# Seven half-size products in place of eight for the forget and query projections and for the second gate

## The chip, the cores and the metric

The kernel runs on one core of one Trainium2 chip. The metric is device time in microseconds, the median of several runs; for the kernel before it is 1528.08 us over three runs (1526.75 to 1529.6).

## The reference

The reference is two layers of a streaming encoder. They work on 288 tokens, 256 of a prompt and 32 of a second request. What matters here is the combined projection at the head of each layer and what its parts feed:

```python
proj = x @ lp['w_in']                       # x: 288 x 1024
cq, ckv, kr, f_pre, q_pre, i_pre, g_pre, ga, gb = split(proj)
# widths: 384, 256, 32, 512 (f), 512 (q), 512 (i), 512 (g), 1024 (ga), 1024 (gb)
log_f = logaddexp(log(lb), log1p(-lb) + log_sigmoid(f_pre))
k = (1 - lb) * sigmoid(-f_pre);  q = silu(q_pre);  v = i_pre      # the recurrence's inputs
merged = sigmoid(ga) * (A @ w_br_a) + sigmoid(gb) * (B @ w_br_b)  # A attention, B recurrence
x = LN1(alpha * x + merged @ w_out)
x = LN2(alpha * x + hierarchical_moe(x) + sigmoid(x @ w_ple_gate) * (p @ w_ple))
```

All data are float32. After the mixers each layer has 32 experts, whose weights (three matrices of 1024 x 512 each) are all read from HBM.

## The kernel before

Every engine has one instruction stream written out by hand, and semaphores order them. A *job* is one filling of a PSUM bank: `tensor_jobs`, `gated_tensor_jobs`, `MIX_JOBS` and `expert_jobs` list the jobs in TensorE's order, and `Book` gives each a number and a bank (the first list goes round the 8 banks; in the second, the side jobs of the gates use banks 6 and 7 in turn). `job_done` waits until TensorE has finished a job, `job_read` until its bank has been emptied.

The normalised input stands turned in `xT` (128 partitions x 8 chunks x 288 tokens). Weights come in *pieces* of 1 MB (128 partitions x 4 chunks x 512 columns, half of the 1024 input rows by 512 outputs) into an 8-slot ring. SyncE issues their loads in the order of `weight_pieces`, each waiting for the last job that used the piece before it in the slot (`last_use`).

- **Forget and query** (f, q). Four jobs each, one for every 128 outputs: `by_features` runs 8 matmuls (the 8 chunks of input) of 128 x 128 weights with 288 tokens. ScalarE takes Sigmoid and Abs of f straight from the bank (L1693, L1694), then Exp and Ln; VectorE ends the logarithm (L2119); in the second layer more steps follow for the lower bound. q goes through Silu (L1726).
- **Gates** (ga, gb). Eight such jobs each. `GATE_AT` strews them between the jobs of the recurrence, where TensorE would otherwise wait: after which job of tile t they stand is the key. ScalarE copies each bank away (L1721), and before the branches `gate_values` takes the Sigmoid of two gates at a time.
- **Recurrence.** For tiles t = 0, 1, 2 VectorE builds decays by levels, and TensorE multiplies them, jobs ("A", t, j), then turns k ("ks", t), then makes the outputs ("o", t) and the new state ("Sn", t). VectorE empties these in tile order; L2292 to L2308 and `whole_products` (L2271 to L2273) stand at a tile's end.
- **Branches, mix, experts.** The branches multiply the gates (`mT`); w_out and the router follow. When the last chunk of `mT` is done (`mg_out`), SyncE starts to load expert weights into the arena, and from then on through the layer one load after another is issued as slots come free.

GpSimd issues the small transfers: norms, caches, the two mask rows of queries and keys (which wait for `lf_out`, since the scratch `fw` lies on the keys' place), states.

## Time and profile before

| | us |
|---|---|
| median of three runs | 1528.08 |
| lowest, highest | 1526.75, 1529.6 |
| the profiled execution, its own time | 1529.54 |
| span of its trace | 1527.7 |
| TensorE busy | 1284.0 (84%) |
| VectorE busy | 404.1 (26%) |
| ScalarE busy | 284.9 (19%) |
| GpSimd busy | 54.1 (4%) |

The span is the stretch from the first to the last instruction of the profiled core. PE is TensorE's matmuls, PEld its weight loads, DVE VectorE, ACT ScalarE, POOL GpSimd, SP SyncE. Every float32 matmul of the program makes two records in the trace: 8 matmuls of a gate job are 16 records. A row of the timeline merges neighbours of one kind, and its length runs to the end of the last; since matmuls are pipelined, the pace of a group is read from its start to the start of the next row.

### The profile page before, as it was taken

The numbers are of one execution on the slowest core, as the hardware profiler recorded it, in microseconds if no ns is written. First come the engines' busy times: TensorE is split into PE (matmuls) and PEld (weight loads), VectorE is DVE, ScalarE is ACT, GpSimd is POOL, SyncE is SP. The second block draws the span as 40 slices with busy tenths as digits, with TensorE's granted clock in tenths as the row PEclk, the third lists the DMA queues.
The fourth block names the chain that finished last, engine by engine and source line by source line (L and its number), as shares of the span: only waits on it lengthen the run. The fifth ranks groups of instructions, "written<-read, shape, count | busy, mean of one in ns | idle before, by whom it ended". The sixth has DMA issues, their size and how long they took to land.

```text
span 1527.7 us, 20304 instructions
## 1 busy us (share of the span) xinstructions
PE 1284.0 (84%) x8528; PEld 722.5 (47%) x8529; DVE 404.1 (26%) x1027; ACT 284.9 (19%) x712; POOL 54.1 (4%) x94
## 2 busy tenths in 40 slices
PE   6999999999787767766799999999997787667665
PEld 4766887554332323322276678876342323223211
DVE  4242643542111101011133536245311111011003
ACT  2342522021001101001044434312111011010001
POOL 1300000000000000000022010000000000000000
PEclk9999999999999878788899999999998988788778
DMA  9503435999999999999972043469999999999994
GB/s 332 162 3 111 173 117 181 386 371 430 430 429 429 430 430 430 430 429 428 383 250 84 6 148 130 179 231 410 369 429 430 431 431 429 431 427 432 430 424 183
DMA packets 79951, 488.78 MB, mean 320 GB/s; under 512 B 7344, under 2 KB 13424, under 8 KB 49776
## 3 DMA queue, kind: packets, MB, share of 16 engines
q1 hardware_dynamic: 75392, 476.47, 75.8%
q0 software_dynamic: 4464, 10.93, 2.3%
q8 instruction: 73, 1.20, 0.3%
q14 instruction: 22, 0.18, 0.0%
HBM read 484.48 MB, written 2.89 MB: 319 GB/s over the span
## 4 chain that ended last, share of the span: by engine, by line
PE 61%; DMA 33%; SPq 2%; DVE 2%; issue 1%; ACT 0%; POOL 0%; DVEq 0%
PE bank L1036 59%; DMA ring<-in_w_e_down 10%; DMA arena<-in_w_e_up 6%; DMA ring<-in_w_e_up 5%; DMA ring<-in_w_e_gate 5%; DMA arena<-in_w_e_gate 4%; DMA arena<-in_w_e_down 2%; PE bank L1086 2%; SPq L872 2%; DMA ring<-in_w_in 1%; DVE arena L2043 0%; SPq L933 0%; DVE x_sb L2052 0%; ACT xT L1644 0%; PE bank L1481 0%
## 5 line engine op out<-in xcount | busy, mean ns | idle before, releaser
L1036 PE MATMUL bank<-arena 128*32 128x512 f32 (+11 forms) x2808 | 570.6, 538 | 175.6 <-DMA ring<-in_w_e_up 51.0
L1036 PE MATMUL bank<-ring,arena 128*32 128x512 f32 (+4 forms) x1360 | 420.4, 647 | 33.4 <-DMA arena<-in_w_e_gate 15.4
L1036 PEld LDWEIGHTS bank<-arena 128*32 128x32 f32 (+6 forms) x2808 | 210.1, 137 | 442.2 <-issue 428.8
L1036 PE MATMUL bank<-ring,xT 128*32 128x128 f32 (+5 forms) x1536 | 237.7, 364 | 1.5 <-ACT xT L1644 1.1
L1036 PE MATMUL bank<-xT,ring 128*128 128x288 f32 x768 | 191.8, 407 | 0.0
L1036 PEld LDWEIGHTS bank<-ring,xT 128*32 128x32 f32 (+1 forms) x1536 | 121.7, 137 | 101.1 <-issue 90.9
L1036 PEld LDWEIGHTS bank<-ring,arena 128*32 128x32 f32 (+1 forms) x1360 | 108.0, 130 | 121.1 <-issue 114.4
L1036 PEld LDWEIGHTS bank<-xT,ring 128*128 128x128 f32 x768 | 143.7, 190 | 37.9
L1036 PE MATMUL bank<-arena,x_sb 128*128 128x128 f32 (+1 forms) x768 | 99.7, 282 | 1.4 <-DVE arena L2375 0.8
L1036 PEld LDWEIGHTS bank<-arena,x_sb 128*128 128x128 f32 (+1 forms) x768 | 90.5, 190 | 19.4 <-issue 12.7
L1036 PE MATMUL bank<-cst,arena 128*32 128x512 f32 x144 | 91.0, 792 | 0.0
L2548 DVE TENSOR_TENSOR arena<-arena,bank 128x512 f32<-128x512 f32 x16 | 11.0, 688 | 241.5 <-PE bank L1036 241.5
L1036 PE MATMUL bank<-arena,ring 128*128 128x288 f32 (+2 forms) x352 | 72.9, 372 | 0.0
L1036 PE MATMUL bank<-lb,arena 128*32 128x512 f32 x144 | 64.8, 592 | 0.0
L1036 PEld LDWEIGHTS bank<-arena,ring 128*128 128x128 f32 (+1 forms) x352 | 56.3, 180 | 14.8 <-issue 0.4
L2555 DVE COPY arena<-bank 128x512 f32<-128x512 f32 x16 | 11.1, 692 | 194.2 <-PE bank L1036 194.2
L1932 ACT COPY arena<-bank 128x512 f32<-128x512 f32 x16 | 9.4, 586 | 232.1 <-PE bank L1036 231.9
L2375 DVE TENSOR_TENSOR arena<-small,arena 128x128 f32<-128x128 f32 (+1 forms) x42 | 9.6, 283 | 147.7 <-PE bank L1036 147.7
L2485 DVE TENSOR_TENSOR arena<-arena,bank 128x512 f32<-128x512 f32 (+1 forms) x64 | 39.3, 630 | 23.2 <-PE bank L1036 23.2
L1985 ACT COPY arena<-bank 128x512 f32<-128x512 f32 x16 | 9.4, 587 | 172.6 <-PE bank L1036 172.6
L1969 ACT ACTIVATE arena<-bank 128x512 f32<-128x512 f32 x16 | 9.6, 597 | 156.1 <-PE bank L1036 156.1
L2421 DVE COPY arena<-bank 128x512 f32<-128x512 f32 x16 | 11.1, 692 | 80.3 <-PE bank L1036 80.3
(232 smaller groups left out, 878.4 us busy)
## 6 DMA issues: line engine op xcount, KB each, us to landing
arena<-in_w_e_up SPq DMA_DIRECT2D x30, 2048.0 KB, 28.2
arena<-in_w_e_gate SPq DMA_DIRECT2D x28, 2048.0 KB, 27.0
ring<-in_w_e_gate SPq DMA_DIRECT2D x24, 2048.0 KB, 25.6
arena<-in_w_e_down SPq DMA_DIRECT2D x20, 2048.0 KB, 23.7
ring<-in_w_e_down SPq DMA_DIRECT2D x18, 2048.0 KB, 25.1
ring<-in_w_in SPq DMA_DIRECT2D x32, 1024.0 KB, 8.7
ring<-in_w_e_up SPq DMA_DIRECT2D x16, 2048.0 KB, 24.0
arena<-in_w_e_gate SPq DMA_DIRECT2D x16, 1024.0 KB, 14.3
```

The costliest lines, as they stand in the source:

```text
L872: sp.dma_start(slot(n)[:, D * c:D * c + D], src).then_inc(last_full if c else ring_full[SLOT_OF[n]], 16)
L1036: return pe.matmul(out, lhsT, rhs, start=first, stop=last, skip_group_check=True)
L1086: ins = pe.transpose(b[0:m, a:a + src.shape[0]], src, ident[0:src.shape[0], 0:src.shape[0]])
L1932: emptied(act.copy(xeT[:, 0:4, :], bank(key)[:, :].rearrange("p (c t) -> p c t", c=4)), key)
L1969: emptied(act.activation(eh[:, :], bank(key)[:, :], ACT.Silu), key)
L1985: emptied(act.copy(ye[0], bank(key)[:, :]), key)
L2375: return dve.tensor_tensor(s4, bcast(places[0:n, :], 1, QUAD), bcast(ranks, 2, CAP), ALU.is_equal)
L2421: emptied(dve.tensor_copy(xeT[:, 4:8, :], bank(key)[:, :].rearrange("p (c t) -> p c t", c=4)), key)
L2485: emptied(dve.tensor_tensor(a, a, src, ALU.add), key)
L2548: emptied(dve.tensor_tensor(hid[:, :], eh[:, :], bank(key)[:, :], ALU.mult), key)
L2555: emptied(dve.tensor_copy(ye[1], bank(key)[:, :]), key)
```

## The change

For the pair f, q and for gb alone the product of a 2 x 2 block of weights (output half j, input half h) with a 2 x 2 block of tokens (token half i of 144, input half) is done in the Strassen-Winograd form, by seven products of half size instead of eight:

- VectorE makes four differences of token quarters after the input has been turned: `xb`, `xa`, `xd` and `xc` (in two parts), 576 elements a partition each. They lie in `lb` and in the free part of `lnw`, and both groups use them.
- Three products use weights as loaded (m = 4, 5, 3) and four use sums of pieces (m = 2, 1, 7, 6). Each product is two jobs (p = 0, 1) of 2 x 4 matmuls with 144 tokens.
- f and q: the four sums (2048 elements a partition each) are made by VectorE in the ring's slots, in place.
- gb: the four sums are made by transfers that add to their destination, issued by GpSimd: two from `w_in` in HBM, two from another slot of the ring. Each of the last three waits for the product that still reads the old content, and the last two wait for the sum before them.
- The products are gathered in SBUF. ScalarE copies m = 4 (twice), 5 and 3; VectorE then adds or subtracts the others' banks, one or two operations each (`gather`). Sigmoid, Abs and Silu work on the gathered f (`fz`) and q.
- ga's four pieces come before gb's four in the order of loads. The order of ScalarE's and VectorE's work after f and q is other: turned latents are read before the logarithm is ended. GpSimd's mask transfers no longer wait for `lf_out`.

The diff, cut:

```diff
+SEVEN = (4, 5, 3, 2, 1, 7, 6)
+SEVEN_WEIGHTS = {1: (1, 1), 2: (0, 0), 3: (1, 0), 4: (0, 0), 5: (1, 1), 6: (1, 0), 7: (0, 1)}
+SEVEN_LAST = {(0, 0): 1, (0, 1): 7, (1, 0): 6, (1, 1): 6}
+SUMS = (2, 7, 1, 6)
+SEVEN_TO = {5: ((0, 0, "subtract"),), 3: ((0, 1, "add"),), 2: ((1, 0, "add"), (1, 1, "subtract")),
+            7: ((0, 0, "add"),), 1: ((0, 0, "add"), (1, 1, "add")), 6: ((1, 1, "add"),)}
...
 GATE_AT = {("ss",): [("ga", 0), ("ga", 1)], ("lat",): [("ga", 2)],
            ("A", 0, 1): [("ga", 3)], ("A", 0, 3): [("ga", 4)], ("ks", 0): [("ga", 5)], ("o", 0): [("ga", 6)],
-           ("A", 1, 1): [("ga", 7)], ("A", 1, 3): [("gb", 0)], ("ks", 1): [("gb", 1)], ("o", 1): [("gb", 2)],
-           ("A", 2, 0): [("gb", 3), ("gb", 4)], ("ks", 2): [("gb", 5)], ("o", 2): [("gb", 6), ("gb", 7)]}
+           ("A", 1, 1): [("ga", 7)], ("A", 1, 3): seven_of("gb", 4), ("ks", 1): seven_of("gb", 5), ("o", 1): seven_of("gb", 3),
+           ("A", 2, 0): seven_of("gb", 2, 1), ("ks", 2): seven_of("gb", 7), ("o", 2): seven_of("gb", 6)}
...
-    for j in range(2):
-        out += [("ga", j, 0), ("ga", j, 1), ("gb", j, 0), ("gb", j, 1)]
+    out += [(name, j, h) for name in ("ga", "gb") for j in range(2) for h in range(2)]
...
-    j += [(name, h) for name in ("f", "q") for h in range(HH)]
+    j += seven_of("fq", *SEVEN)
...
-        return (name, HH - 1)
+        return ("fq", SEVEN_LAST["fq".index(name), key[1]], 1)
...
+        def quarter(i, k):
+            return xT[:, 4 * k:4 * k + 4, S * i:S * i + S]
...
+        xa = tiles(lbr[:, 40:40 + 4 * S])
+        xb = tiles(lbr[:, 40 + 4 * S:40 + 8 * S])
+        xc_parts = [tiles(lbr[:, 40 + 8 * S:40 + 10 * S]), tiles(early[:, 4 * T:4 * T + 2 * S])]
+        xd = tiles(early[:, 4 * T + 2 * S:4 * T + 6 * S])
+        whole = lambda a: [a[:, c, :] for c in range(4)]
+        seven_tokens = {1: whole(xa), 2: whole(quarter(1, 1)), 3: whole(quarter(0, 0)), 4: whole(xb), 5: whole(quarter(0, 1)),
+                        6: [part[:, c, :] for part in xc_parts for c in range(2)], 7: whole(xd)}
+        def seven_out(name, i, j, p):
+            pair = gate_pair(FEATURES // 2 + 2 * j + p).rearrange("p (u t) -> p u t", u=2) if name == "gb" else (fz, hqT)[j][:, 2 * p:2 * p + 2, :]
+            return pair[:, :, S * i:S * i + S]
...
-                pool.wait_ge(lf_out, 2 * layer + 2)
...
+                ns = {(j, h): piece_number(layer, ("gb", j, h)) for j in range(2) for h in range(2)}
+                w = {at: slot(n).rearrange("p (c n) -> p c n", c=4) for at, n in ns.items()}
+                def from_input(j, h):
+                    a = OFF["gb"][0] + 512 * j
+                    return w_in[layer].rearrange("(p c) n -> p c n", c=8)[:, 4 * h:4 * h + 4, a:a + 512]
                 job_read(pool, (layer, "aTs"))
                 pool.dma_start(state[1][:, :, :], state_hgrn[layer, 0].rearrange("h k v -> k h v")).then_inc(state_in, 16)
+                pool.wait_ge(ring_full[SIGNAL_OF[ns[0, 1]]], 16 * FILLS[ns[0, 1]])
+                pool.dma_start(w[0, 1], from_input(1, 1), accum_op=ALU.add).then_inc(gb_sum[7], 16)
+                job_done(pool, (layer, "gb", 4, 1))
+                pool.dma_start(w[0, 0], from_input(0, 1), accum_op=ALU.add).then_inc(gb_sum[2], 16)
+                job_done(pool, (layer, "gb", 5, 1))
+                pool.wait_ge(gb_sum[2], 16 * (layer + 1))
+                pool.dma_start(w[1, 1], w[0, 0], accum_op=ALU.add).then_inc(gb_sum[1], 16)
+                job_done(pool, (layer, "gb", 3, 1))
+                pool.wait_ge(gb_sum[1], 16 * (layer + 1))
+                pool.dma_start(w[1, 0], w[1, 1], accum_op=ALU.add).then_inc(gb_sum[6], 16)
...
+                def seven(key, n):
+                    m, p = key[-2:]
+                    arrived(n)
+                    pe.wait_ge(forms_out, layer + 1)
+                    if key[1] == "gb" and m in SUMS:
+                        pe.wait_ge(gb_sum[m], 16 * (layer + 1))
+                    if key[1] == "fq" and m in SUMS:
+                        pe.wait_ge(fq_sums, 4 * layer + SUMS.index(m) + 1)
+                    w = slot(n).rearrange("p (c n) -> p c n", c=4)
+                    b = open_bank(key)
+                    for u in range(2):
+                        f = 2 * p + u
+                        for c in range(4):
+                            ins = mm(b[:, S * u:S * u + S], w[:, c, P * f:P * f + P], seven_tokens[m][c], c == 0, c == 3)
+                    done(ins)
...
-                for name in ("f", "q"):
-                    for h in range(HH):
-                        by_features(layer, (name, h), h, [(name, 0), (name, 1)], xT)
+                for name, m, p in seven_of("fq", *SEVEN):
+                    j, h = SEVEN_WEIGHTS[m]
+                    seven((layer, name, m, p), piece_number(layer, ("fq"[j], h)))
...
-                for h in range(HH):
-                    job_read(pe, (layer, "q", h))
+                pe.wait_ge(hq_out, layer + 1)
...
+                def seven_copies(key, signal):
+                    name, m, p = key[1:]
                     job_done(act, key)
-                    z = bank(key)[:, 0:T]
-                    act.activation(hk[:, h, :], z, ACT.Sigmoid, scale=-1.0)
-                    ins = act.activation(lf[:, h, :], z, ACT.Abs)
-                step(ins)
+                    if m == 4:
+                        act.copy(seven_out(name, 0, 0, p), seven_bank(key))
+                        emptied(act.copy(seven_out(name, 1, 0, p), seven_bank(key)), key)
+                    else:
+                        act.copy(seven_out(name, 0 if m == 5 else 1, 1, p), seven_bank(key)).then_inc(signal, 1)
+                for key in seven_of("fq", 4, 5, 3):
+                    seven_copies((layer,) + key, fq_copied)
+                act.wait_ge(fq_out, 2 * layer + 1)
+                act.activation(hk[:, :, :], fz[:, :, :], ACT.Sigmoid, scale=-1.0)
+                step(act.activation(lf[:, :, :], fz[:, :, :], ACT.Abs))
...
+                act.wait_ge(fq_out, 2 * layer + 2)
+                act.activation(hqT[:, :, :], hqT[:, :, :], ACT.Silu).then_inc(hq_out, 1)
...
+                step(dve.tensor_tensor(xb, quarter(1, 0), quarter(1, 1), ALU.subtract))
+                step(dve.tensor_tensor(xa, quarter(0, 0), xb, ALU.subtract))
+                dve.tensor_tensor(xd, quarter(0, 1), xa, ALU.subtract)
+                dve.tensor_tensor(xc_parts[0], quarter(1, 0)[:, 0:2, :], quarter(0, 0)[:, 0:2, :], ALU.subtract)
+                dve.tensor_tensor(xc_parts[1], quarter(1, 0)[:, 2:4, :], quarter(0, 0)[:, 2:4, :], ALU.subtract).then_inc(forms_out, 1)
+                def gather(key, signal):
+                    name, m, p = key[1:]
+                    job_done(dve, key)
+                    if m in (5, 3):
+                        dve.wait_ge(signal, copied(layer, m, p))
+                    job_read(dve, (layer, name, SEVEN[SEVEN.index(m) - 1], p))
+                    for i, j, op in SEVEN_TO[m]:
+                        g = seven_out(name, i, j, p)
+                        ins = dve.tensor_tensor(g, g, seven_bank(key), {"add": ALU.add, "subtract": ALU.subtract}[op])
+                    return emptied(ins, key)
...
+                js = {(j, h): piece_number(layer, ("fq"[j], h)) for j in range(2) for h in range(2)}
+                for n in (js[0, 1], js[1, 1]):
+                    dve.wait_ge(ring_full[SIGNAL_OF[n]], 16 * FILLS[n])
+                w = {at: slot(n) for at, n in js.items()}
+                job_done(dve, (layer, "fq", 4, 1))
+                dve.tensor_tensor(w[0, 0], w[0, 0], w[0, 1], ALU.add).then_inc(fq_sums, 1)
+                dve.wait_ge(fq_sums, 4 * layer + 1)
+                dve.tensor_tensor(w[0, 1], w[0, 1], w[1, 1], ALU.add).then_inc(fq_sums, 1)
+                gather((layer, "fq", 5, 0), fq_copied)
+                gather((layer, "fq", 5, 1), fq_copied)
+                dve.wait_ge(fq_sums, 4 * layer + 2)
+                dve.tensor_tensor(w[1, 1], w[0, 0], w[1, 1], ALU.add).then_inc(fq_sums, 1)
+                gather((layer, "fq", 3, 0), fq_copied)
+                gather((layer, "fq", 3, 1), fq_copied)
+                dve.wait_ge(fq_sums, 4 * layer + 3)
+                dve.tensor_tensor(w[1, 0], w[1, 0], w[1, 1], ALU.add).then_inc(fq_sums, 1)
+                for m in (2, 1, 7, 6):
+                    for p in range(2):
+                        gather((layer, "fq", m, p), fq_copied)
+                    if m in (7, 6):
+                        for p in range(2):
+                            job_read(dve, (layer, "fq", m, p))
+                        dve.sem_inc(fq_out, 1)
...
+                    gates_at("A", t, j)
...
+                    gates_at("ks", t)
+                    gates_at("o", t)
```

Where the orders differ. First TensorE at the start of f and q; a row is line, operation, output bank <- operands, size, and the semaphores waited for. Before:

```order
L1036 MATMUL bank<-xT,ring 128x288 [waits ring_full4,bank_emptied4]
L1036 MATMUL bank<-xT,ring 128x288 x3
L1036 MATMUL bank<-xT,ring 128x288 [waits ring_full5]
L1036 MATMUL bank<-xT,ring 128x288 x3
L1036 MATMUL bank<-xT,ring 128x288 [waits ring_full4,bank_emptied5]
L1036 MATMUL bank<-xT,ring 128x288 x3
```

In the changed kernel, from the second job of m = 4 to the first of m = 2 (`lb` holds xb; forms_out is the token differences, fq_sums VectorE's sums of weights):

```order
L1105 MATMUL bank<-lb,ring 128x144 [waits bank_emptied5,forms_out,ring_full4]
L1105 MATMUL bank<-lb,ring 128x144 x7
L1105 MATMUL bank<-xT,ring 128x144 [waits bank_emptied6,forms_out,ring_full7]
L1105 MATMUL bank<-xT,ring 128x144 x7
L1105 MATMUL bank<-xT,ring 128x144 [waits bank_emptied7,forms_out,ring_full7]
L1105 MATMUL bank<-xT,ring 128x144 x7
L1105 MATMUL bank<-xT,ring 128x144 [waits bank_emptied0,forms_out,ring_full6]
L1105 MATMUL bank<-xT,ring 128x144 x7
L1105 MATMUL bank<-xT,ring 128x144 [waits bank_emptied1,forms_out,ring_full6]
L1105 MATMUL bank<-xT,ring 128x144 x7
L1105 MATMUL bank<-xT,ring 128x144 [waits fq_sums,bank_emptied2,forms_out,ring_full4]
L1105 MATMUL bank<-xT,ring 128x144 x7
```

A job of 8 matmuls with 288 tokens has become a job of 8 with 144. From m = 2 on (the first row with fq_sums) a product waits for a sum. The first list of jobs is six longer now, so its banks shift: ("A", 0, 0), the first job of the second list, takes the bank that ("g", 2), two jobs earlier, has filled; before it was the bank of ("ga", 2).

VectorE at the same place. Before, after the third tile's latents it had four operations for f and then the turned latents:

```order
L2102 SCALAR_TENSOR_TENSOR arena<-arena,small 32x256 [waits kr_out]
L2119 SCALAR_TENSOR_TENSOR arena<-bank,arena 128x288 [waits f_act]
L2119 SCALAR_TENSOR_TENSOR arena<-bank,arena 128x288
L2119 SCALAR_TENSOR_TENSOR arena<-bank,arena 128x288 [waits bank_emptied4,bank_emptied5,f_act]
L2119 SCALAR_TENSOR_TENSOR arena<-bank,arena 128x288
L2145 COPY arena<-bank 128x3x128 [waits bank_emptied6,bank_emptied7,matmuls_done]
```

Now the four sums over `ring` stand there, with the gathers between them:

```order
L2229 SCALAR_TENSOR_TENSOR arena<-arena,small 32x256 [waits kr_out]
L2246 TENSOR_TENSOR ring<-ring 128x2048 [waits matmuls_done,ring_full7,ring_full5]
L2248 TENSOR_TENSOR ring<-ring 128x2048 [waits fq_sums]
L2213 TENSOR_TENSOR arena<-arena,bank 128x2x144 [waits bank_emptied4,fq_copied,matmuls_done]
L2213 TENSOR_TENSOR arena<-arena,bank 128x2x144 [waits bank_emptied5,fq_copied,matmuls_done]
L2252 TENSOR_TENSOR ring<-ring 128x2048 [waits fq_sums]
L2213 TENSOR_TENSOR arena<-arena,bank 128x2x144 [waits bank_emptied6,fq_copied,matmuls_done]
L2213 TENSOR_TENSOR arena<-arena,bank 128x2x144 [waits bank_emptied7,fq_copied,matmuls_done]
L2256 TENSOR_TENSOR ring<-ring 128x2048 [waits fq_sums]
L2213 TENSOR_TENSOR arena<-arena,bank 128x2x144 [waits bank_emptied0,matmuls_done]
L2213 TENSOR_TENSOR arena<-arena,bank 128x2x144
L2213 TENSOR_TENSOR arena<-arena,bank 128x2x144 [waits bank_emptied1,matmuls_done]
```

The first sum waits for a matmul job (m = 4 done) and for two pieces; each gather waits for its product and for ScalarE's copy.

TensorE at the second gate, between the recurrence's ("Sn", 1) and ("A", 2, 0). Before, two gate jobs:

```order
L1036 MATMUL bank<-xT,ring 128x288 [waits ring_full2,bank_emptied6]
L1036 MATMUL bank<-xT,ring 128x288 x3
L1036 MATMUL bank<-xT,ring 128x288 [waits ring_full3]
L1036 MATMUL bank<-xT,ring 128x288 x3
L1036 MATMUL bank<-xT,ring 128x288 [waits ring_full6,bank_emptied7]
L1036 MATMUL bank<-xT,ring 128x288 x3
L1036 MATMUL bank<-xT,ring 128x288 [waits ring_full7]
L1036 MATMUL bank<-xT,ring 128x288 x3
```

Now the products m = 2 and m = 1, two jobs each, in banks 7, 6, 7, 6:

```order
L1105 MATMUL bank<-xT,ring 128x144 [waits gb_sum_2,bank_emptied7,forms_out,ring_full4]
L1105 MATMUL bank<-xT,ring 128x144 x7
L1105 MATMUL bank<-xT,ring 128x144 [waits gb_sum_2,bank_emptied6,forms_out,ring_full4]
L1105 MATMUL bank<-xT,ring 128x144 x7
L1105 MATMUL bank<-lb,ring 128x144 [waits gb_sum_1,bank_emptied7,forms_out,ring_full7]
L1105 MATMUL bank<-lb,ring 128x144 x7
L1105 MATMUL bank<-lb,ring 128x144 [waits gb_sum_1,bank_emptied6,forms_out,ring_full7]
L1105 MATMUL bank<-lb,ring 128x144 x7
```

The third job wants the bank that the first of them filled: VectorE must have gathered it. gb_sum_2 and gb_sum_1 are the adding transfers.

## Rows read from the trace of the kernel before

**Rows 1.** the page's part 4, shares of the chain that ended last

```profile
PE 61%; DMA 33%; SPq 2%; DVE 2%; issue 1%; ACT 0%; POOL 0%; DVEq 0%
PE bank L1036 59%; DMA ring<-in_w_e_down 10%; DMA arena<-in_w_e_up 6%; DMA ring<-in_w_e_up 5%; DMA ring<-in_w_e_gate 5%; DMA arena<-in_w_e_gate 4%; DMA arena<-in_w_e_down 2%; PE bank L1086 2%; SPq L872 2%; DMA ring<-in_w_in 1%; DVE arena L2043 0%; SPq L933 0%; DVE x_sb L2052 0%; ACT xT L1644 0%; PE bank L1481 0%
```

**Rows 2.** stretches A:B; length, busy us of PE and others, then PE clock, DMA share, GB/s

```profile
38.50:69.64 31.14, 31.14 (x133) 24.43 (x129) 3.84 (x14) 12.40 (x26) 12.47 (x24) 1.00 0.44 134
409.00:768.00 359.00, 261.00 (x1717) 107.17 (x1710) 50.10 (x98) 33.55 (x60) 0.00 (x0) 0.85 1.00 424
```

**Rows 3.** timeline of SP, which issues the weight loads: start, us, transfers

```profile
269.65 5.10 SPq L806 DMA_DIRECT2D arena<-in_w_e_gate  x8
```

**Rows 4.** timeline of PE: start us, us, engine, line, operation, tiles, shape, count

```profile
38.50 31.31 PE L1036 MATMUL bank<-xT,ring 128*128 128x288 f32 x128
69.64 2.60 PE L1086 MATMUL bank<-cst,arena 128*128 128x128 f32 x18
...
98.28 2.02 PE L1036 MATMUL bank<-arena 98*128 98x128 f32 x16 [0.36 <-DVE arena L2167]
...
165.54 3.68 PE L1036 MATMUL bank<-arena 128*128 128x64 f32 x32
169.06 4.10 PE L1036 MATMUL bank<-xT,ring 128*128 128x288 f32 x16
...
183.73 2.84 PE L1036 MATMUL bank<-arena 128*128 128x128 f32 x24
186.41 3.80 PE L1036 MATMUL bank<-xT,ring 128*128 128x288 f32 x15
```

**Rows 5.** timeline of PE, first layer, where the second gate's jobs stand

```profile
194.25 4.05 PE L1036 MATMUL bank<-xT,ring 128*128 128x288 f32 x16
...
200.57 4.15 PE L1036 MATMUL bank<-xT,ring 128*128 128x288 f32 x16
...
211.55 7.93 PE L1036 MATMUL bank<-xT,ring 128*128 128x288 f32 x32
...
225.78 7.93 PE L1036 MATMUL bank<-xT,ring 128*128 128x288 f32 x32
233.64 3.13 PE L1036 MATMUL bank<-arena 32*32 32x128 f32 x24
```

**Rows 6.** timeline of VectorE, whose additions and outputs stand beside those jobs

```profile
32.21 0.61 DVE L2093 SCALAR_TENSOR_TENSOR arena<-arena,small 32x384 f32<-32x384 f32 x1 [1.44 <-ACT small L1630]
...
212.60 1.13 DVE L2292 SCALAR_TENSOR_TENSOR arena<-bank,small,arena 128x128 f32<-128x128 f32 x4 [9.99 <-ACT small L1630]
...
215.93 0.28 DVE L2273 TENSOR_TENSOR arena<-arena 128x128 f32<-128x128 f32 x1
...
240.33 0.46 DVE L2322 TENSOR_TENSOR xT<-lnw,bank 128x288 f32<-128x288 f32 x1
...
817.00 0.76 DVE L2137 TENSOR_TENSOR arena<-arena 128x576 f32<-128x576 f32 x1 [1.23 <-ACT arena L1707]
```

**Rows 7.** timeline of all engines at the last jobs of the attention

```profile
159.73 1.11 ACT L1713 ACTIVATE arena<-bank 32x128 f32<-32x128 f32 x4 [1.33 <-PE bank L1036]
160.66 0.97 PEld L1036 LDWEIGHTS bank<-arena 128*128 128x128 f32 x8
```

**Rows 8.** DMA issues of three stretches: line, queue, count, KB each, median us to landing

```profile
ring<-in_w_in SPq DMA_DIRECT2D x4, 1024.0 KB, 8.1
...
ring<-in_w_ple_gate SPq DMA_DIRECT2D x2, 1024.0 KB, 6.4
lnw<-in_ln_g POOLq DMA_DIRECT2D x1, 512.0 KB, 4.5
arena<-in_p_prompt POOLq DMA_DIRECT2D x1, 256.0 KB, 3.0
...
ring<-in_w_in SPq DMA_DIRECT2D x4, 1024.0 KB, 10.3
arena<-in_state_hgrn POOLq DMA_DIRECT2D x1, 256.0 KB, 6.9
```

More of the change, by code:

```diff
@@ L319, in last_use @@
         return (name,) + LATE_PLAIN[3]
-    if name in ("ga", "gb", "bra", "brb"):
+    if name == "gb":
+        return (name, SEVEN_LAST[key[1:]], 1)
+    if name in ("ga", "bra", "brb"):
         return (name, 4 * key[1] + 3)
@@ L509, in build @@
         hg = carve(H + 6144, 3, 512)
+        fz = carve(H + 6144, HH, T)
         squares = carve(0, 512)
@@ L667, in build @@
         more_read = sem("more_read")
+        forms_out = sem("forms_out")
+        fq_sums = sem("fq_sums")
+        fq_copied = sem("fq_copied")
+        fq_out = sem("fq_out")
+        hq_out = sem("hq_out")
+        gb_sum = {m: sem(f"gb_sum_{m}") for m in SUMS}
+        gb_copied = sem("gb_copied")
         block = ctx.enter_context(nc.Block())
@@ L684, in bank, with seven_bank, copied @@
             return banks[book.bank(key)]
+        def seven_bank(key):
+            return bank(key)[:, 0:T].rearrange("p (u t) -> p u t", u=2)
+        def copied(layer, m, p):
+            return 4 * layer + 2 * (m == 3) + p + 1
         def further_passes(eng, layer, turn, body, each_pass=None):
@@ L1700, in _ @@
                     act.activation(z, z, ACT.Ln, bias=1.0).then_inc(f_act, 1)
+                for t in range(3):
+                    key = (layer, "kvT", t)
+                    job_done(act, key)
+                    src = bank(key)[:, 0:256].rearrange("p (c t) -> p c t", c=2)[:, :, 0:NT[t]]
+                    emptied(act.copy(ckvT[:, :, T0[t]:T0[t] + NT[t]], src), key)
                 if layer == 1:
@@ L2095, in _, with gates_at @@
                 for t in range(3):
+                    job_read(dve, (layer, "tx", t, 1))
+                step(dve.tensor_tensor(xb, quarter(1, 0), quarter(1, 1), ALU.subtract))
[13 more added lines that the diff above has]
+                    return emptied(ins, key)
+                def gates_at(*place):
+                    for name, *f in GATE_AT.get(place, []):
+                        if name == "gb" and f[0] != 4:
+                            gather((layer, name, *f), gb_copied)
+                for t in range(3):
                     key = (layer, "kv", t)
@@ L2133, in _ @@
-                if layer == 1:
-                    for i in range(2):
-                        z = lf[:, 2 * i:2 * i + 2, :]
-                        dve.wait_ge(f_add, i + 1)
-                        dve.tensor_tensor(z, z, fw[:, 2 * i:2 * i + 2, :], ALU.add).then_inc(lf_out, 1)
-                    dve.wait_ge(lf_out, 2 * layer + 2)
+                js = {(j, h): piece_number(layer, ("fq"[j], h)) for j in range(2) for h in range(2)}
+                for n in (js[0, 1], js[1, 1]):
+                    dve.wait_ge(ring_full[SIGNAL_OF[n]], 16 * FILLS[n])
@@ L2273, in whole_products @@
                     dve.tensor_tensor(ksufT[:, :, 0:n], ksufT[:, :, 0:n], hk[:, :, now(t)], ALU.mult).then_inc(ksuf_out, 1)
-                for h in range(HH):
-                    job_read(dve, (layer, "q", h))
+                dve.wait_ge(hq_out, layer + 1)
                 dve.wait_ge(zeroed, 3 * layer + 4)
```

85 lines of the change are left out of this document (46 added, 39 removed).

## The prediction

> **What bounds the kernel now.** I read the page's chain first. It gives 61% of the span to TensorE and 33% to transfers, nearly all of them expert weights [rows 1]. The two do not mix: they are stages. Then the stretches: from 409 to 768 us, in the experts, the DMA share is 1.00 at 424 GB/s while TensorE is busy for 261 of 359 us; at the f and q projections (38.50 to 69.64) TensorE is busy for all 31.14 us at granted clock 1.00 and the DMA share is 0.44 [rows 2]. So the dense stages are TensorE's and the expert stages the transfers'. What links them is the point from which expert weights are issued, 269.65 us in the first layer [rows 3], which follows the last chunk of the merged gates, so TensorE's dense work. Whatever the dense work before it loses, the stream starts earlier by, and as it then runs without a gap, the layer ends earlier by as much. The second layer is alike. A microsecond of TensorE saved in f, q or gb is therefore worth a microsecond.
>
> **Products.** 64 matmuls with 288 tokens, 128 records, take 69.64 - 38.50 = 31.14 us for f and q [rows 4], 243 ns a record. That is 288 columns at two cycles of 2.4 GHz (240 ns) and some 3 ns. A gate job of 16 records has the same pace (225.78 to 233.64 for two jobs, 7.86 us; I use 3.88 a job) [rows 5]. So eight gate jobs are 8 x 3.88 = 31.0 us. Afterwards each is 7 x 2 x 8 = 112 matmuls with 144 tokens, 224 records.
>
> The trace has no 144-column matmul. With so few columns the weight load (128 columns) could bound it, so I look at its floor: 32 records of 64 columns take 169.06 - 165.54 = 3.52 us, 110 ns each, though 64 columns alone would be 53; 24 records of 128 columns take 186.41 - 183.73 = 2.68 us, 112 ns [rows 4]. The loads run beside the matmuls and bound them at about 111 ns. 144 columns want 120 + 3 = 123 ns, which is above it. So 224 x 123 = 27.5 us. I take that; the lower bound of the saving is the case that an overhead appears (a rival below). The f/q group saves 31.14 - 27.5 = 3.6 us, gb 31.0 - 27.5 = 3.5 us, per layer.
>
> The Trainium skill says otherwise: in "TensorE: Matmul & The Clock Gate", section "Back-to-back issue gap", a stream of load and matmul pairs is paced by both, 81 ns at N = 128 against 56 for the matmul alone, 25 ns more; and the section on the array's mechanism lets a load overlap only with other row groups. By it, as an estimate, a record here is 123 + 25 = 148 ns, a group 33.2 us, and seven products lose 2 us against eight. The trace disagrees: at 128 columns its records stand 112 ns apart where two cycles a column alone are 107.
>
> **f and q: what must be hidden.** Each product m takes 32 x 123 = 3.9 us: from 38.5, m = 4 ends at 42.4, 5 at 46.4, 3 at 50.3, 2 at 54.2, 1 at 58.1, 7 at 62.1, 6 at 66.0.
> - *Token differences.* 576 elements cost VectorE 0.76 us, 288 about 0.45 [rows 6]: 3 x 0.76 + 2 x 0.43, some 3.3 us with their waits. They follow the operation that ends at 32.82 [rows 6] and end near 36.2, before 38.5. Cost 0, spare 2.3 us; beyond that TensorE waits.
> - *Weight sums.* 2048 elements by the slope from 288 to 576 elements (0.46, 0.76: about 1.05 ns an element) are 2.3 us. Two start when m = 4 is done: 42.5 to 47.1. The first is wanted at 50.3. Two gathers, then the third, 48.1 to 50.4, wanted at 54.2. The fourth, 51.3 to 53.6, wanted at 62.1. Each has at least 3.8 us to spare. In the second layer the steps of the lower bound stand ahead of the first sum, a few operations and two waits for ScalarE; its 5.5 us should hold them. Cost 0 in both.
> - *Gathers.* 12 jobs of one or two additions at 0.46: each job's work is under 1 us against 1.96 us of its matmuls; the banks come round after eight jobs. Cost 0.
> - *The logarithm.* f is whole only after m = 7, 4 us before the group's end, where half of it was read before. ScalarE's chain on it (in the second layer the longer one) now runs beside the turned latents, i and the query's up-projection, whose copies queue behind it on ScalarE. TensorE has 98.28 - 69.64 = 28.6 us of jobs before the first scores [rows 4], and ScalarE only these copies. Cost 0; if that fails, what is late are the first scores, where VectorE's copies of the keys stand in between anyway. I allow 1 us a layer.
>
> **gb: two new kinds of wait.** *VectorE as the one that empties banks.* Until m = 2 each product has a slot as long as a gate job had, so TensorE's times stay: m = 4 from 194.25, 5 from 200.6, 3 from 205, 2 from 211.6. Its first job is done at 213.6, and the first job of m = 1 wants the bank back at 215.6. But VectorE works at the outputs of tile 1 from 212.60 until 216.21 [rows 6], and the gather stands behind that: two additions, 217.1. TensorE waits 1.5 us. Behind the waiting job are ("A", 2, 0) and all that follows. No other gather is late.
> *The shifted bank.* ("A", 0, 0) now wants the bank of ("g", 2), which ScalarE empties at 159.73 + 1.11 = 160.84 [rows 7]; TensorE starts that job at 160.66 now [rows 7]. 0.2 us.
> *The adding transfers.* Let T be the time from issue to landing of one. Three form a chain: from m = 4's end (198.2) for m = 2 (wanted 211.6), then for m = 1 (217.1), then for m = 6 (226 + 1.5 = 227.5). The first needs T up to 13.4; two need 2T up to 18.9; three, 3T up to 29.3. So T up to 9.4 us costs nothing. The trace has no such transfer. Bounds: a plain 1 MB issued by SP lands after 6.4 to 10.3 us where several queue; GpSimd's 256 KB lands after 3.0, its 512 KB after 4.5 us [rows 8], which by their slope is 7.5 us for a plain 1 MB. Far above lies its 256 KB in 6.9 us among the gate's own loads [rows 8]; four times that is 27.6. Below: at the 424 GB/s of [rows 2] the data take 2.5 us and some 2.3 us are fixed, 4.8. An adding transfer also reads its destination, 2.5 us more: 7.3. I take 7.5, near the rows for 256 and 512 KB, which no queue held up. So no wait.
> The Trainium skill ("Collectives: The Full Stack", "The bandwidth ceiling: the fold count and why AG ≠ RS ≠ AR") says that the add itself costs nothing but that there are two source reads, which halve the rate; as an estimate that is the same 7.3 us, and no row here shows it.
>
> **Sum.** Per layer 3.6 + 3.5 - 1.5 - 0.2 = 5.4; both layers, 10.8 us. The profiled execution took 1529.54 us (its span 1527.7), 1.5 above the median of the runs. 1529.54 - 10.8 = 1518.7; against the median, 1528.08 - 10.8 = **1517.3 us**.
>
> **Rivals.**
> 1. *The adding transfers are the bound; slower.* Past T = 9.7 the last sum is late by 3T - 29.3 in each layer. The kernel is as before when this eats 5.4 us: T = 11.6. At T = 14 it waits 12.7 us a layer: 1528.1 - 10.8 + 25.4 = 1543. For it: GpSimd's 6.9 us for 256 KB; nobody here has seen adding. Against it: the bus has room there (TensorE's stage at f and q had a DMA share of 0.44 [rows 2], and no expert load runs), and the 3.0 us. 0.21 for T over 11, of which 0.02 up to 12.
> 2. *144 columns pay an overhead; no difference.* At 135 ns a record (12 over my figure) a group is 30.2 us and saves 0.8 to 0.9; with the waits, 4 x 0.85 - 3.4 = 0. 1528. For it: the load's floor is only 12 ns below. Against it: the 112 ns. 0.07. The page's 148 ns would give 1528.1 + 8.4 + 3.4 = 1540; 0.02.
> 3. *The bank wait does not come*, since gathers find VectorE free: 1517.3 - 3.0 = 1514.3. Against it stands VectorE's written order. 0.08.
> 4. *The stream does not follow*: the experts' start is bound elsewhere and the gain is lost in part. 1523. The trace has no gap to lose it in. 0.05.
> The forecast itself, with T up to 11: 0.57.
>
> **Numbers.** A difference under 0.2%, 3 us, could not be told from none. The forecast, rivals 3 and 4 are faster: 0.70. Rival 2 and T from 11 to 12 are the same: 0.09. Rival 1 beyond T = 12 and the page's pace are slower: 0.21. The range: down to 1513 (all waits gone), up to 1533 (T about 12.6); about 0.15 lies above and 0.04 below. The forecast's own range is 1514 to 1521.
>
> **What would show it.** Records with 144 columns 122 to 124 ns apart; f and q in 27.5 us with TensorE never idle for `fq_sums`; an idle of about 1.5 us before the first job of m = 1, ended by VectorE; adding transfers landing after about 7.5 us, with no idle ended by them; the first expert load 5.4 us earlier in the first layer and 10.8 in the second. It is wrong if TensorE idles for `gb_sum`, if records stand 135 ns apart, or if the second layer's scores wait for ScalarE.

## The result, and the profile after

The changed kernel takes 1517.59 us, the median of four runs (1516.82 to 1520.38), against 1528.57 for the kernel before on the same chip. The medians lie 10.98 us apart; the ratio of the runs is 0.9933 (95% 0.9919 to 0.9947), which is 10.2 us less (8 to 12). The forecast was 1517.3. The profiled execution took 1517.23 us, its span is 1515.5.

**The page.** Busy time, queue 0 (GpSimd's) and the chain:

```profile
PE 1273.6 (84%) x8912; PEld 738.4 (49%) x8913; DVE 453.6 (30%) x1109; ACT 287.0 (19%) x710; POOL 62.8 (4%) x102
...
q0 software_dynamic: 7152, 19.32, 5.4%
...
PE 57%; DMA 35%; DVE 3%; SPq 3%; issue 1%; ACT 1%; POOL 0%; DVEq 0%
```

TensorE is busy 10.4 us less than before and VectorE 49.5 more. TensorE's share of the chain fell from 61% to 57% [rows 1]. It is still the same chain of stages.

**f and q.** TensorE, start and length of merged groups (m = 4; then 5, 3 and 2 in one row; 1; 7; and m = 6 in small rows):

```profile
37.38 4.19 PE L1105 MATMUL bank<-lb,ring 128*128 128x144 f32 x32
41.41 11.92 PE L1105 MATMUL bank<-xT,ring 128*128 128x144 f32 x96
53.16 4.08 PE L1105 MATMUL bank<-lb,ring 128*128 128x144 f32 x32
57.09 4.08 PE L1105 MATMUL bank<-lnw,ring 128*128 128x144 f32 x32
61.01 0.65 PE L1105 MATMUL bank<-lb,ring 128*128 128x144 f32 x4
...
64.92 1.30 PE L1155 MATMUL bank<-cst,arena 128*128 128x128 f32 x9
```

From 37.38 to 64.92 are 27.54 us for 224 records, 123 ns each, where 128 records took 31.14 [rows 4]. No row has an idle time in brackets.

**The same stretches as [rows 2].** Length, busy time of each engine, granted clock, DMA share, GB/s:

```profile
37.38:64.92 27.54, 27.54 (x230) 27.54 (x225) 17.19 (x29) 9.29 (x21) 12.45 (x24) 1.00 0.53 156
...
409.00:768.00 359.00, 261.69 (x1719) 110.00 (x1719) 53.03 (x101) 34.41 (x63) 0.00 (x0) 0.85 1.00 422
```

**gb.** TensorE, the rows that answer to [rows 5]; in brackets the idle time and what ended it:

```profile
189.82 4.09 PE L1105 MATMUL bank<-lb,ring 128*128 128x144 f32 x32
193.74 2.50 PE L1105 MATMUL bank<-arena 128*128 128x64 f32 x24
196.17 4.19 PE L1105 MATMUL bank<-xT,ring 128*128 128x144 f32 x32
...
207.23 4.09 PE L1105 MATMUL bank<-xT,ring 128*128 128x144 f32 x32
212.77 4.16 PE L1105 MATMUL bank<-lb,ring 128*128 128x144 f32 x32 [1.45 <-DVE arena L2213]
```

The one wait of gb's products is that before m = 1, in the second layer as well:

```profile
957.61 4.16 PE L1105 MATMUL bank<-lb,ring 128*128 128x144 f32 x32 [1.45 <-DVE arena L2213]
```

VectorE at that place, with the outputs of tile 1 (L2443), the state (L2459), the products for tile 2 (L2423), and only then the gathers (L2213), as [rows 6] had it without the last:

```profile
208.28 1.13 DVE L2443 SCALAR_TENSOR_TENSOR arena<-bank,small,arena 128x128 f32<-128x128 f32 x4 [2.58 <-ACT small L1718]
...
210.05 1.11 DVE L2459 SCALAR_TENSOR_TENSOR arena<-arena,small,bank 128x128 f32<-128x128 f32 x4
...
211.62 0.28 DVE L2423 TENSOR_TENSOR arena<-arena 128x128 f32<-128x128 f32 x1
211.82 1.54 DVE L2213 TENSOR_TENSOR arena<-arena,bank 128x288 f32<-128x288 f32 x4
```

**The adding transfers.** GpSimd, the issues for m = 2, 1 and 6 of the first layer and of the second. An issue whose idle time was ended by a DMA started when the sum before it had landed:

```profile
194.33 1.28 POOL L1064 DMA_DIRECT2D ring<-in_w_in  x1 [28.14 <-PE bank L1105]
203.59 0.87 POOL L1067 DMA_DIRECT2D ring<-ring  x1 [7.98 <-DMA ring<-in_w_in]
211.11 0.84 POOL L1070 DMA_DIRECT2D ring<-ring  x1 [6.64 <-DMA ring<-ring]
...
939.19 1.30 POOL L1064 DMA_DIRECT2D ring<-in_w_in  x1 [27.15 <-PE bank L1105]
948.79 0.88 POOL L1067 DMA_DIRECT2D ring<-ring  x1 [8.29 <-DMA ring<-in_w_in]
956.98 0.84 POOL L1070 DMA_DIRECT2D ring<-ring  x1 [7.31 <-DMA ring<-ring]
```

From issue to next issue one link takes 9.26 and 7.52 us in the first layer, 9.60 and 8.19 in the second. From issue to landing it is 8.6 and 6.9, then 8.9 and 7.6; the 0.6 to 0.7 us between are GpSimd's hand-over to the next link. The sum for m = 1 was there at 211.1 and 957.0, against the starts of m = 1 at 212.77 and 957.61. So 1.7 and 0.6 us were left. Without VectorE's wait TensorE would have been ready 1.45 us sooner, at 211.32 and 956.16, so in the second layer the transfer hides behind that wait.

The fourth adding transfer, for m = 7, is off the chain: issued at 164.86 us among SyncE's plain loads of the ring, it landed after 13.6 us (14.5 in the second layer). Its issue, and the GB/s of 170 to 180 us in 40 slices:

```profile
ring<-in_w_in POOLq DMA_DIRECT2D x1, 1024.0 KB, 13.6
...
GB/s 262 262 262 262 262 262 262 262 262 262 262 262 262 262 262 254 287 246 262 262 262 254 246 254 262 254 254 262 254 262 320 385 418 393 426 401 410 385 254 82
```

Beside it the queues moved some 260 GB/s, and about 400 from 177.6 us on, when it was nearly done. Here nobody waited: m = 7 is wanted at 218.92.

**Where the time went.** I cut the span at six events: the start of f and q, the start of the branches and the first expert load, in either layer. From branches to load are 32.94 or 32.95 us in every case. The runs come from several chips, and each ratio is to the kernel before on the same chip, whose median there is 1528.51 to 1529.23 us. All kernels in one table (stretches in us, worked out from the starts of their rows, as 230.36 - 37.38 = 192.98):

| kernel | f/q starts | f/q to branches, layer 0 | load to layer 1's f/q | f/q to branches, layer 1 | last load point to end | median | ratio to before (95%) |
|---|---|---|---|---|---|---|---|
| before | 38.50 | 198.20 | 518.87 | 198.36 | 507.88 | 1528.57 | |
| changed | 37.38 | 192.98 | 518.80 | 193.08 | 507.36 | 1517.59 | 0.9933 (0.9919 to 0.9947) |
| fq_only | 37.86 | 194.87 | 518.83 | 194.97 | 506.77 | 1520.75 | 0.9945 (0.9932 to 0.9959) |
| gb_only | 37.12 | 196.29 | 519.16 | 196.29 | 505.75 | 1522.37 | 0.9957 (0.9944 to 0.9969) |
| early_gather | 37.19 | 191.75 | 519.04 | 191.93 | 505.79 | 1515.41 | 0.9913 (0.9899 to 0.9927) |
| early_gather_7first | 36.97 | 191.29 | 517.47 | 191.40 | 507.17 | 1512.29 | 0.9897 (0.9881 to 0.9912) |
| vector_sums_early | 37.42 | 191.74 | 517.62 | 191.83 | 508.50 | 1515.36 | 0.9915 (0.9902 to 0.9929) |
| sum1_twice | 37.48 | 201.05 | 517.82 | 201.08 | 506.07 | 1532.62 | 1.0020 (1.0009 to 1.0032) |
| sum6_twice | 37.14 | 200.06 | 520.87 | 200.93 | 505.61 | 1531.14 | 1.0013 (1.0004 to 1.0023) |

The two dense stretches give back 5.22 and 5.28 us, 10.5 together. The stretch that ends in the experts is as long as before (518.87, 518.80): the stream follows one for one. SyncE's first expert load answers to [rows 3]:

```profile
263.31 4.30 SPq L858 DMA_DIRECT2D arena<-in_w_e_gate  x8
...
1008.14 4.96 SPq L858 DMA_DIRECT2D arena<-in_w_e_gate  x8
```

6.3 us earlier than before, and 11.7 in the second layer (1019.82 before). Of both, 1.1 us is the earlier start of f and q. Without it they are 5.2 and 10.6, for 5.4 and 10.8 forecast. The start lies between 36.97 and 37.86 in the eight other traces of the table, and at 38.50 only in that of before. All of the 1.1 us arises before the latents of the second tile, which start at 21.73 us before and at 20.62 after; from there to f and q it is 16.77 and 16.76. No edited line runs that early, so I don't count it as the change's.

### The profile page after: what moved, and what is told of

Read it like the earlier page. It is cut to its first block, busy times and chain, and to the rows that moved or that the text cites. A ratio compares the mean times of both kernels' runs of the same rounds, so it can differ in the third digit from the quotient of the medians.

```text
span 1515.5 us, 21258 instructions
## 1 busy us (share of the span) xinstructions
PE 1273.6 (84%) x8912; PEld 738.4 (49%) x8913; DVE 453.6 (30%) x1109; ACT 287.0 (19%) x710; POOL 62.8 (4%) x102
## 4 chain that ended last, share of the span: by engine, by line
PE 57%; DMA 35%; DVE 3%; SPq 3%; issue 1%; ACT 1%; POOL 0%; DVEq 0%
PE bank L1105 55%; DMA ring<-in_w_e_up 7%; DMA ring<-in_w_e_down 5%; DMA ring<-in_w_e_gate 5%; DMA arena<-in_w_e_up 4%; DMA cst<-in_w_e_down 4%; DMA arena<-in_w_e_gate 4%; DMA cst<-in_w_e_gate 3%; DMA arena<-in_w_e_down 2%; SPq L924 2%; PE bank L1155 2%; DMA ring<-in_w_in 1%; SPq L985 0%; DVE arena L2304 0%; DVE arena L2144 0%
## 5 line engine op out<-in xcount | busy, mean ns | idle before, releaser
L1105 PE MATMUL bank<-xT,ring 128*128 128x144 f32 (+1 forms) x640 | 113.4, 335 | 0.0
L1105 PEld LDWEIGHTS bank<-xT,ring 128*128 128x128 f32 x640 | 95.1, 190 | 12.3
L2706 DVE COPY arena<-bank 128x512 f32<-128x512 f32 x16 | 11.1, 692 | 191.5 <-PE bank L1105 191.5
L1105 PE MATMUL bank<-lb,ring 128*128 128x144 f32 x320 | 43.5, 287 | 2.9 <-DVE arena L2213 2.9
L1105 PEld LDWEIGHTS bank<-lb,ring 128*128 128x128 f32 x320 | 40.7, 190 | 3.5 <-issue 3.3
```

The lines of the kernel that those rows point to most:

```text
L1105: return pe.matmul(out, lhsT, rhs, start=first, stop=last, skip_group_check=True)
L2706: emptied(dve.tensor_copy(ye[1], bank(key)[:, :]), key)
```

## The experiments

**One group alone.** fq_only gives gb back to `by_features`, with its order of loads; gb_only gives f and q back.

```diff
-("A", 1, 3): seven_of("gb", 4), ("ks", 1): seven_of("gb", 5), ...
+("A", 1, 3): [("gb", 0)], ("ks", 1): [("gb", 1)], ...        # fq_only
...
-    j += seven_of("fq", *SEVEN)
+    j += [(name, h) for name in ("f", "q") for h in range(HH)]  # gb_only
```

> Seven products for f and q alone; the gate gb is as in the kernel before. Theory (each part pays by its matmul time): f and q again in 27.5 us, 3.6 us less a layer, minus the 0.2 us of the shifted bank: 1528.1 - 6.8 = 1521.3 us, the first expert load 3.4 us earlier in layer 0 and 6.8 in layer 1. Rival (the 1.1 us by which f and q started earlier in the changed kernel's trace, 37.38 against 38.50, belong to the change): f and q start at 37.4 here too and the time is 1520.2. Rival (the gate carries the gain): above 1524.

> Seven products for the gate gb alone, with the adding transfers; f and q are as in the kernel before. Theory: 3.5 us less a layer, minus 1.5 us in which the first product of m = 1 waits for VectorE: 1528.1 - 4.0 = 1524.1 us. With the f and q run this adds up to the changed kernel's 11. Rival (the adding transfers take as much from the loads of the later weights as the products save): 1528. Rival (f and q carry nothing, the gate all): 1517.5.

Measured: 1520.75 and 1522.37 us. The dense stretches are shorter by 3.33 and 3.39 us (fq_only) and by 1.91 and 2.07 (gb_only). Added up that is 5.24 and 5.46, where the whole change has 5.22 and 5.28: the parts are independent, and each is worth its matmul time less its wait. In fq_only 0.25 of the 3.6 is missing, which is the shifted bank; TensorE idles there for 0.25 and 0.24 us in its two layers, as in this row of the changed kernel:

```profile
156.26 1.13 PE L1105 MATMUL bank<-arena 128*128 128x128 f32 x8 [0.25 <-ACT arena L1816]
```

In gb_only the wait for VectorE is the same. The idle time is 1.46 us; from start to start the step takes 5.55 us (215.82 - 210.27) where one without a wait takes 3.93, 1.6 more, and 3.5 - 1.6 is the 1.9 measured:

```profile
215.82 4.16 PE L1106 MATMUL bank<-lb,ring 128*128 128x144 f32 x32 [1.46 <-DVE arena L2219]
```

The early start of f and q is in gb_only too (37.12), whose f and q are the old ones, so it is not theirs. By time the two kernels gain 8.5 and 6.9 us against the median of their chip, 1529.23, more together than the change's 11.0, and gb_only's interval (4.7 to 8.6 us) leaves its 4.0 out. The surplus lies in the start (1.4 us) and after the last load point (2.1 us), where the edit changed nothing that I can name. One trace of the kernel before doesn't tell whether it is scatter; that stays open.

**The wait for VectorE taken away.**

```diff
-                        if name == "gb" and f[0] != 4:
+                        if name == "gb" and f[0] != 4 and f != [2, 0]:
...
                     dve.tensor_tensor(osb[0:n, :], osb[0:n, :], hg[0:n, t, :], ALU.mult).then_inc(o_out, 1)
+                    if t == 1:
+                        gather((layer, "gb", 2, 0), gb_copied)
                     key = (layer, "Sn", t)
```

> The changed kernel, but VectorE gathers the first half of product m = 2 before it updates the state of tile 1 instead of after it (0.8 us of work moved ahead). This takes away the wait of 1.45 us that each layer has before m = 1. Theory (behind that wait stands the chain of adding transfers, which lands for m = 1 at about 211.1 us in layer 0 and 957.0 in layer 1, while TensorE is ready at 211.3 and 956.2): the wait goes in layer 0, and in layer 1 some 0.8 us of it stay, now ended by the transfer: 1517.6 - 2.1 = 1515.5 us. Rival (VectorE is all there is to the wait): 1517.6 - 2.9 = 1514.7, no wait ended by a transfer. Rival (what follows on TensorE waits for VectorE anyway): 1517.6.

TensorE at m = 1, in both layers:

```profile
210.96 2.12 PE L1105 MATMUL bank<-lb,ring 128*128 128x144 f32 x16
213.31 2.20 PE L1105 MATMUL bank<-lb,ring 128*128 128x144 f32 x16 [0.23 <-DVE arena L2213]
...
955.28 4.16 PE L1105 MATMUL bank<-lb,ring 128*128 128x144 f32 x32 [0.33 <-DMA ring<-ring]
```

1515.41 us; the stretches lose 1.23 and 1.15. In the second layer the wait is now the transfer's, 0.33 us (0.8 expected). In the first, 0.23 stays for the second half's gather. The theory stands: behind the one wait stood another. By time alone the gain isn't clear of noise: this interval (0.9899 to 0.9927) and the changed kernel's (0.9919 to 0.9947) overlap a little. The two waits in the traces carry the reading.

**Another order, which gives the chain room.**

```diff
+GB_SEVEN = (4, 5, 3, 7, 2, 1, 6)
-("A", 2, 0): seven_of("gb", 2, 1), ("ks", 2): seven_of("gb", 7),
+("A", 2, 0): seven_of("gb", 7, 2), ("ks", 2): seven_of("gb", 1),
```

The gather moved ahead is that of m = 7, and gates of the first half wait for m = 1 in place of 7.

> The early gather kernel with another order of the gate's products: 4, 5, 3, 7, 2, 1, 6 in place of 4, 5, 3, 2, 1, 7, 6. The sum for m = 7 is ready long before, so each sum of the chain of adding transfers is wanted a product (3.9 us and more) later. Theory (in layer 1 what was left of the wait, 0.33 us, was the chain's): no wait ended by a transfer in either layer; from the start of f and q to the branches 191.8 us in layer 0 (as with the early gather) and 191.6 in layer 1 (191.9 there); 1515.1 us. Rival (the order is no matter, TensorE waits for VectorE's gathers alone): 191.8 and 191.9. Rival (m = 1 now stands where VectorE is late with the attention's last parts): a new wait of a microsecond, 1517.

```profile
206.83 4.09 PE L1106 MATMUL bank<-lnw,ring 128*128 128x144 f32 x32
...
952.57 4.08 PE L1106 MATMUL bank<-xT,ring 128*128 128x144 f32 x32
```

No wait is left between gb's products in either layer: 191.29 and 191.40 us, 0.5 and 0.2 under the theory. It had left the first layer's wait for VectorE in place, and that went too: a gather of m = 7 is one addition where m = 2 has two, so VectorE is done with the second half at 212.22 us, before TensorE wants the bank, and not at 213.16. 1512.29 us; the interval (0.9881 to 0.9912) lies below that of the change (0.9919 to 0.9947). It is the fastest of all, and beats both kernels; against the early gather the intervals overlap, and of the 3.1 us between the medians 1.0 is in the dense stretches. Of the 5.3 us against the changed kernel 3.4 are in the dense stretches; 1.3 are in the first layer's experts. That stretch runs from 517.47 to 520.87 us in the table, though no edit touches it, so the 1.3 are put down to scatter.

**The sums on VectorE.** The early gather with gb's sums made in the slots by VectorE:

```diff
-                pool.dma_start(w[1, 1], w[0, 0], accum_op=ALU.add).then_inc(gb_sum[1], 16)
...
+                                dve.tensor_tensor(gw[to], gw[a], gw[b], ALU.add).then_inc(gb_sum[m], 1)
```

> The early gather kernel with the gate's four weight sums on VectorE, between its gathers, in place of adding transfers. Theory (the transfers cost nothing where they land in time, and VectorE has gaps of 1.5 to 2.6 us between the gathers that hold most of 2.3 us a sum): the stretch from f and q to the branches is 191.4 to 191.9 us in both layers, 1515 us, the same as the early gather. Rival (the transfers take bandwidth from the loads beside them): shorter, 1513. Rival (four sums of 2.3 us in VectorE's order make the recurrence's steps late): TensorE waits 1 to 2 us a layer, ended by VectorE, 1518.

The first of VectorE's sums, behind a gather (L2195); the others are alike:

```profile
198.95 0.45 DVE L2195 TENSOR_TENSOR arena<-arena,bank 128x288 f32<-128x288 f32 x1 [0.35 <-ACT arena L1767]
199.32 2.28 DVE L2218 TENSOR_TENSOR ring<-ring 128x2048 f32<-128x2048 f32 x1
```

1515.36 us, stretches of 191.74 and 191.83 against 191.75 and 191.93: the same. So the transfers cost no time where they land in time. They do take from the loads beside them, as that rival had it: SyncE's two pieces of `w_br_a`, issued at 161 us, land after 18.6 us in the early gather kernel and after 13.7 here:

```profile
ring<-in_w_br_a SPq DMA_DIRECT2D x2, 1024.0 KB, 18.6
...
ring<-in_w_br_a SPq DMA_DIRECT2D x2, 1024.0 KB, 13.7
```

TensorE doesn't wait for them in either kernel, so the 5 us don't show in the stretches. VectorE had room for four sums, and is the surer place: all eight took 2.28 us.

**The chain made longer.** The transfer for m = 1 twice, then in another kernel that for m = 6:

```diff
                 pool.dma_start(w[1, 1], w[0, 0], accum_op=ALU.add).then_inc(gb_sum[1], 16)
+                pool.wait_ge(gb_sum[1], 32 * layer + 16)
+                pool.dma_start(w[1, 1], w[0, 0], accum_op=ALU.add).then_inc(gb_sum[1], 16)
...
```

> The changed kernel with the adding transfer for m = 1 issued twice, one behind the other (so the sum for m = 1 holds one piece twice). The chain is one transfer longer. Theory (a transfer lands 7.2 to 9.4 us after its issue, and the chain has under 2 us to spare before m = 1): the sum lands at about 218.5 in layer 0 and 964.5 in layer 1, and TensorE, which starts m = 1 at 212.8 and 957.6, waits some 6 more us in each; m = 6 waits for nothing more: 1517.6 + 12 = 1530 us. Rival (there is slack of a whole transfer, as my forecast of 7.5 us and 9.7 at most would have it in part: 3 x 7.5 = 22.5 against 18.9): + 3.6 us a layer, 1524.8. Rival (the second one costs only its data's time, 5 us): 1517.6 + 2 x 3.5 = 1524.6.

```profile
218.13 6.97 PE L1107 MATMUL bank<-lb,ring 128*128 128x144 f32 x32 [6.73 <-DMA ring<-ring]
...
970.85 6.10 PE L1107 MATMUL bank<-lb,ring 128*128 128x144 f32 x32 [7.53 <-DMA ring<-ring]
```

The theory has the waits (m = 1 starts 5.3 and 6.0 us later in its stretch than in the changed kernel), but 1532.62 us is 2.6 above its 1530. The same 32 records that took 4.16 us now take 6.97 and 6.10. The stretches say why (the column before the last two is the granted clock):

```profile
218.13:225.03 6.90, 6.90 (x32) 6.76 (x32) 0.82 (x2) 0.00 (x0) 1.64 (x2) 0.58 0.79 157
225.03:231.40 6.37, 6.37 (x89) 6.27 (x89) 2.95 (x10) 0.59 (x1) 0.00 (x0) 1.00 0.62 205
```

After 6.7 us of idleness the granted clock is 0.58 over the product, so TensorE was for the most part at its lower level, 1.2 GHz, and at 2.4 again (1.00) in the next stretch. So of the 8.07 us by which the first layer's dense stretch is longer than the changed kernel's, 5.3 are the wait and 2.8 the clock.

> The changed kernel with the last adding transfer, the one for m = 6, issued twice, one behind the other (so the sum for m = 6 holds one piece twice). In the changed kernel its issue stands at 211.1 us in layer 0 and 957.0 in layer 1 and it lands some 7.3 us later, where TensorE wants it at 223.3 and 968.1. Theory (the last sum has 4.9 and 3.8 us to spare): it lands at 225.8 and 971.7, TensorE waits 2.5 and 3.6 us ended by the transfer, and if so short a wait leaves the granted clock at 1.00 the time is 1517.6 + 6.1 = 1523.7 us. Rival (the clock falls as in the run with the transfer for m = 1 doubled, where 16 records of a product took about twice their time): + 2 us and more a layer, 1528. Rival (the last sum has a whole transfer's room): 1517.6.

```profile
227.69 1.30 PE L1107 MATMUL bank<-lb,ring 128*128 128x144 f32 x4 [4.35 <-DMA ring<-ring]
...
232.57 0.65 PE L1107 MATMUL bank<-lnw,ring 128*128 128x144 f32 x4
```

```profile
227.69:232.57 4.88, 4.88 (x20) 4.88 (x21) 0.46 (x1) 0.00 (x0) 0.00 (x0) 0.51 0.45 172
```

Here the theory failed and its rival was right, and still too low: 1531.14 us, 13.5 above the changed kernel. TensorE waited 4.35 and 5.64 us where 2.5 and 3.6 were expected, since the second of the two landed after 8.9 and 9.2 us where the first took 7.6 and 7.2. Beside the second ran a 256 KB store and SyncE's loads of `w_out` (the row is the first layer's); that they made it late is likely but not shown by a run of its own:

```profile
216.85 6.45 SPq L858 DMA_DIRECT2D ring<-in_w_out  x2
```

Then TensorE ran 20 and 16 records at some 245 ns (granted clock 0.51 and 0.50) instead of 123: 2.4 and 2.0 us more.

**How near the weight load is.**

```diff
+                            cols = 96 if key[1] == "fq" and c else S
-                            ins = mm(b[:, S * u:S * u + S], ..., seven_tokens[m][c], c == 0, c == 3)
+                            ins = mm(b[:, S * u:S * u + cols], ..., seven_tokens[m][c][:, 0:cols], c == 0, c == 3)
```

> The changed kernel; of the four matmuls of each sum of the f and q products the first keeps its 144 tokens and the other three take only 96 of them (48 of each 144 tokens get a quarter of the product only). It shows how near 144 columns are to the bound by the weight load. Theory (a record takes the longer of its columns, 96 x 2 cycles and 3 ns = 83 ns, and the load's floor of 111 ns): 56 records at 123 and 168 at 111 ns, 25.5 us, against 27.54. Rival (loads bound nothing, only columns count): 20.8 us. Rival (load and matmul add up in part, so that 144 columns carry some of the load too): above 26.

```profile
37.52 3.90 PE L1105 MATMUL bank<-lb,ring 128*128 128x144 f32 x32
...
63.22 2.61 PE L1155 MATMUL bank<-cst,arena 128*128 128x128 f32 x18
```

25.70 us, near the theory's 25.5. With 56 records at 123 the other 168 took 112 ns each, as those of 64 and 128 columns did (110 and 112) [rows 4]. The first matmul keeps its 144 tokens because with all four at 96 part of each bank would stay unwritten; that form gave no time. A third fewer columns buys 11 ns of 123. In the second layer it is 25.7 us again, and the one run of this kernel took 1513.97 us.

## Why the forecast was right

Its sum was 5.4 us a layer, 10.8; the dense stretches lost 5.22 and 5.28. That the time came within 0.3 us of the forecast is luck: the four runs spread over 3.6 us. By its steps:

- **Products at 123 ns, not 135 or 148.** Measured 123: 27.54 us against 27.5. Two cycles a column and 3 ns were right, and so was the floor from the 64- and 128-column rows (112 ns again). The Trainium skill ("TensorE: Matmul & The Clock Gate", "Back-to-back issue gap") says that both the load and the matmul set the pace, 81 ns at 128 columns where a matmul alone has 56. Carried over to these records that was an estimate of 148 ns, and they disagree with it.
- **The wait for VectorE, 1.5 us.** Measured 1.45 in both layers, at the place named (1.6 from start to start), and it went, but for what the transfer and the second half's gather still cost, when the gather was moved. The third rival (no wait) fell. The shifted bank: 0.25 for 0.2.
- **f and q hidden.** Right. The sum for m = 1 had less to spare than was said (at least 3.8 us) in the second layer. VectorE there:

```profile
788.45 2.29 DVE L2246 TENSOR_TENSOR ring<-ring 128x2048 f32<-128x2048 f32 x1
...
793.71 2.29 DVE L2252 TENSOR_TENSOR ring<-ring 128x2048 f32<-128x2048 f32 x1
```

It ended at 796.0, and TensorE began m = 1 at 797.89: 1.9 us. The size of a sum, 2.3 us, was right. No wait for ScalarE's logarithm came up before the first scores.
- **The adding transfers: the term that was mis-sized.** With T = 7.5 from issue to landing, the first two links were to use 15 us. They used 17.4 and 18.4 (from the end of m = 4, 193.74 and 938.57, to the issues at 211.11 and 956.98). The landings are 15.5 and 16.5 of that: 8.6 and 8.9 us from HBM, 6.9 and 7.6 between slots. The other 1.9 us are three hand-overs by GpSimd, 0.6 to 0.7 us each, which the sum put at nothing. The limit for two, 18.9 us, was right (212.77 - 193.74 = 19.0). The forecast held by 0.6 us in the second layer, and only because VectorE's wait came last. My estimate took 424 GB/s for both reads and a fixed 2.3 us. The DMA rows of 194 to 203 us (40 slices: busy share in tenths, GB/s) show the link from HBM:

```profile
DMA  0000000000995699699999999999999999985000
GB/s 0 0 0 0 0 0 0 0 0 0 82 64 55 82 146 164 118 173 228 200 218 182 209 182 218 209 209 209 191 209 200 218 218 200 218 146 100 9 0 0
```

Some 2 us pass, then the queues are busy for 6.2 us, at about 210 GB/s, but at 55 to 173 in the first 1.8. The Trainium skill ("Collectives: The Full Stack", "The bandwidth ceiling: the fold count and why AG ≠ RS ≠ AR") says that an add needs two source reads, which halve the rate; the trace agrees, with 210 against the 424 GB/s of [rows 2]. GpSimd's queue is not what halves it: its plain loads, alone on the queues from 246.7 to 248.0 us of the changed kernel, ran at some 400 GB/s. What neither gave is the slow beginning.
- **The stream follows.** 518.87 and 518.80 us; the fourth rival fell.
- **The first rival's price was too low.** It counted late sums as waits alone. The doubled transfers show that a wait of 4 to 7 us also costs 2.0 to 2.8 us of slower clock. By its formula T = 11 is 3.7 us too late, which with some 2 us of clock would have eaten the layer's 5.2 (an estimate from these numbers). Such a T is in the same trace: the sum for m = 7, issued among other loads, took 13.6 and 14.5 us. Beside the chain's first two links GpSimd's queue was all but alone, as the forecast held against this rival. Two slips of the formula changed nothing: past T = 9.45 the second link would be late first (2T against 18.9), and T = 12.6 makes 1534, not 1533.
